# Tokens to the experts and back: row tables in DRAM with indirect transfers instead of products with selection matrices

## The chip, the cores and the metric

The kernel runs on one core of one Trainium2 chip; the other cores do nothing. The metric is the device time of one execution in microseconds. Before the change the median of three runs is 1745.82 us (1745.56 to 1750.58).

## What is computed

Two decoder layers over 256 tokens of width 1024. Each layer has a mixer (a state-space part, attention and a gated delta rule, with one projection in and one out), a layer norm, a feed-forward part and another layer norm. The feed-forward part is dense in layer 0 (width 3584). In layer 1 it is a mixture of 8 experts of the same size, and each token goes to its two best:

```python
def swiglu(x, w_gate, w_up, w_down):
    return (jax.nn.silu(x @ w_gate) * (x @ w_up)) @ w_down

def moe_ffn(x, router_w, w_gate, w_up, w_down):
    logits = (x @ router_w).astype(F32)
    top_val, top_idx = lax.top_k(logits, TOP_K)
    gates = jax.nn.softmax(top_val, axis=-1)
    combine = jnp.sum(jax.nn.one_hot(top_idx, N_EXPERTS, dtype=F32) * gates[..., None], axis=-2)
    out = jnp.zeros(x.shape, F32)
    for e in range(N_EXPERTS):
        out = out + combine[..., e:e + 1] * swiglu(x, w_gate[e], w_up[e], w_down[e]).astype(F32)
    return out.astype(x.dtype)
```

The layer ends with `layer_norm(DEEPNORM_ALPHA * x + f, ...)`, where `f` is this output.

## The kernel before

Each engine has its own program, and all order between them is written out by hand with semaphores. The change lies in the expert part of layer 1, and in one place of SP's queue in layer 0.

**The channel mixer** (one function per engine, each named `channel_mixer`) runs once for the dense layer (`i is None`, both blocks of 128 tokens) and once per expert `i` (one block of at most 128 gathered tokens). The weights of a layer or an expert come in 42 pieces of 1 MB (`SEQ`): for each of 7 strips `j` of 512 hidden columns two gate pieces (G), two up pieces (U) and, one strip later, two down pieces (D). SP loads piece `r` into one of 7 raw buffers (`next_piece`, L415) as soon as the low part of the piece seven before it has been taken. A float32 weight is used as a sum of two parts: ScalarE writes the high part (`high_part`, L581), VectorE the low part as raw minus high (`low_part`, L950), each into one of three buffers that become free when TensorE has used the piece three before. TensorE makes three products (high by high, low by high, high by low) for each pair of tiles: `inward` (L1361) for G and U, `outward` (L1373) for D; for an expert that is 12 products of 128x512 per piece. After the gate pieces ScalarE takes silu (L612), VectorE multiplies with the up product to `h` (L982), TensorE turns it with four transposes (L1435), and ScalarE and VectorE write its two parts (L618, L1005).

**The router** (L1244 to L1275) finds each token's two experts, their weights (`comb`) and each token's place among those of its expert (`pos`, from products with a triangle of ones, L1751 to L1755). `count_i` holds the largest number of tokens of an expert; only if it is over 128 a second pass over the experts runs.

**Tokens to an expert.** VectorE compares a row of 0..127 with `pos` and gets a selection matrix `pick` (L957). TensorE multiplies the two parts of x (`xs`, written by L770 and L1229) with it, 16 products per part (`gather`, L1344), which gives the expert's tokens already turned; ScalarE and VectorE copy them out as `xg` (L590, L963). For expert i+1 both gathers stand inside expert i, the first after piece 35, the second after piece 39. TensorE also turns `pick` once per expert (L1443), and ScalarE copies it (L621).

**Back to the tokens.** At an expert's end ScalarE and VectorE write two parts of its output (`ye`, L603, L988), TensorE multiplies them with the turned `pick` (8 products, L1458), and VectorE adds the result times `comb` to x (L996). x was scaled by ALPHA before, on POOL (L569). The last layer norm follows (L927 to L939).

**SP's queue in layer 0** (L433 to L438): the mixer's weights, the first 7 pieces of the dense layer (`first_pieces`, L410; pieces 4 and 5 wait until half of the output projection has been used, piece 6 until the projection is done), then pieces 7 to 41, then the mixer's weights of layer 1.

## Time and profile before

| | |
|---|---|
| median of three runs | 1745.82 us |
| profiled execution: its time, its span | 1748.89 us, 1746.7 us |
| TensorE busy | 1638.8 us (94%) |
| VectorE busy | 1297.2 us (74%) |
| ScalarE busy | 935.4 us (54%) |
| POOL busy | 155.4 us (9%) |
| mean granted TensorE clock | 0.968 of 2.4 GHz |
| moved by DMA | 440.14 MB, mean 252 GB/s |

An engine's busy time is a mean over stages that are limited by different things. The dense layer takes TensorE from 227 to 464 us, the experts from 709 to 1731 us. In rows of a timeline the columns are start, duration, engine, line, operation, output and input, count, and in brackets the idle time before with what ended it. A row of busy time by windows has the stretch, its length, the busy time (instructions) of PE, PEld, DVE, ACT and POOL, the granted clock, the DMA share and GB/s. PEld is TensorE's weight load, SPq an issue of SP's DMA queue. A TensorE clock of 1.00 is 2.4 GHz, of 0.50 is 1.2 GHz.

### The profile page before, as it was taken

What the parts mean: (1) busy time and instruction counts of PE and PEld (TensorE: products, weight loads), DVE (VectorE), ACT (ScalarE), POOL (GpSimd) and SP (SyncE); (2) the same over time, 40 slices, a digit from 0 to 9 for tenths busy, and PEclk for the clock granted to TensorE, in tenths of its full rate; (3) what the DMA queues carried; (4) which work ended last, traced back from release to release, by engine and by line L of the source; (5) the groups of instructions that cost most, each with busy time, mean ns of one, the idle gap of its engine ahead of it and who ended that gap; (6) DMA issues with size and microseconds to landing.
All of it is one profiled execution on the core that took longest, in us unless ns stands there. A gap on an engine that the chain in (4) does not pass through costs nothing.

```text
span 1746.7 us, 23280 instructions
## 1 busy us (share of the span) xinstructions
PE 1638.8 (94%) x8938; PEld 1330.4 (76%) x8938; DVE 1297.2 (74%) x1219; ACT 935.4 (54%) x778; POOL 155.4 (9%) x169
## 2 busy tenths in 40 slices
PE   7978989999899697999999999999999999999996
PEld 6857578888787474788788788787887887887885
DVE  7776655444528566588888888888888888887886
ACT  1233234433202421577676776777776776776773
POOL 0342074000015211000000000000000000000000
PEclk9988999999999898899999999999999999999998
DMA  8430156554443104599899899898998998998991
GB/s 315 146 121 3 49 194 216 192 177 162 162 146 125 44 3 169 178 375 360 298 374 359 294 374 343 324 376 315 353 372 319 337 371 322 350 373 295 365 378 51
DMA packets 183982, 440.14 MB, mean 252 GB/s; under 512 B 6576, under 2 KB 8752, under 8 KB 183152
## 3 DMA queue, kind: packets, MB, share of 16 engines
q1 hardware_dynamic: 182640, 431.15, 68.4%
q0 software_dynamic: 1280, 8.15, 1.2%
q8 instruction: 41, 0.67, 0.2%
q14 instruction: 21, 0.17, 0.0%
HBM read 438.22 MB, written 1.05 MB: 251 GB/s over the span
## 4 chain that ended last, share of the span: by engine, by line
PE 81%; DVE 11%; ACT 4%; issue 4%; DMA 1%; DVEq 0%; SPq 0%
PE ps L1361 41%; PE ps L1373 21%; PE ps L1320 5%; PE ps L1680 3%; PE ps L1344 2%; PE ps L1435 2%; ACT hi L581 2%; DVE arena L1053 1%; PE ps L1327 1%; PE ps L1458 1%; PE ps L1650 1%; DMA arena<-in_w_in 1%; PE ps L1636 1%; DVE small L927 1%; DVE arena L907 1%
## 5 line engine op out<-in xcount | busy, mean ns | idle before, releaser
L950 DVE TENSOR_TENSOR lo<-arena,hi 128x2048 fp32r<-128x2048 f32 x378 | 871.3, 2307 | 254.6 <-ACT hi L581 254.5
L581 ACT ACTIVATE hi<-arena 128x2048 fp32r<-128x2048 f32 x378 | 723.9, 1918 | 421.2 <-PE ps L1361 291.0
L1361 PE MATMUL ps<-hi,xg 128*128 128x512 f32 x1792 | 557.8, 393 | 1.5 <-DVE xg L963 1.5
L1361 PEld LDWEIGHTS ps<-hi,xg 128*128 128x128 f32 x1792 | 337.4, 189 | 71.4 <-issue 1.7
L1361 PE MATMUL ps<-lo,xg 128*128 128x512 f32 x896 | 350.3, 391 | 0.0
L1373 PE MATMUL ps<-hi,hTe 128*128 128x512 f32 x896 | 282.5, 396 | 0.7
L1361 PEld LDWEIGHTS ps<-lo,xg 128*128 128x128 f32 x896 | 169.3, 189 | 35.9
L1373 PEld LDWEIGHTS ps<-hi,hTe 128*128 128x128 f32 x896 | 164.0, 188 | 33.4 <-issue 1.6
L1373 PE MATMUL ps<-lo,hTe 128*128 128x512 f32 x448 | 175.0, 391 | 0.0
L1361 PE MATMUL ps<-hi,xs 128*128 128x512 f32 x448 | 138.8, 391 | 0.5 <-issue 0.5
L1320 PE MATMUL ps<-arena 128*128 128x256 f32 x544 | 121.6, 386 | 3.9 <-DMA arena<-in_w_in 2.8
L1320 PEld LDWEIGHTS ps<-arena 128*128 128x128 f32 x544 | 105.4, 194 | 19.9 <-issue 4.6
L1373 PEld LDWEIGHTS ps<-lo,hTe 128*128 128x128 f32 x448 | 84.2, 188 | 18.8
L1361 PEld LDWEIGHTS ps<-hi,xs 128*128 128x128 f32 x448 | 84.4, 189 | 18.2 <-issue 0.9
L1361 PE MATMUL ps<-lo,xs 128*128 128x512 f32 x224 | 87.4, 390 | 0.0
L643 ACT ACTIVATE arena<-ps 128x512 f32<-128x512 f32 (+2 forms) x22 | 12.3, 558 | 124.3 <-PE ps L1320 98.8
L1373 PE MATMUL ps<-hi,hTd 128*128 128x512 f32 x224 | 69.5, 391 | 0.0
L1680 PE MATMUL ps<-arena 128*128 128x512 f32 x128 | 58.1, 602 | 2.6 <-DVE arena L1157 2.6
L982 DVE TENSOR_TENSOR arena<-ps,arena 128x512 f32<-128x512 f32 (+1 forms) x63 | 46.9, 744 | 5.7 <-PE ps L1361 5.7
L1361 PEld LDWEIGHTS ps<-lo,xs 128*128 128x128 f32 x224 | 42.2, 188 | 8.8
L1373 PEld LDWEIGHTS ps<-hi,hTd 128*128 128x128 f32 x224 | 41.6, 188 | 8.3
L1680 PEld LDWEIGHTS ps<-arena 128*128 128x128 f32 x128 | 23.3, 190 | 29.2 <-issue 24.9
(327 smaller groups left out, 1509.5 us busy)
## 6 DMA issues: line engine op xcount, KB each, us to landing
arena<-in_mg SPq DMA_DIRECT2D x112, 1024.0 KB, 5.1
arena<-in_mu SPq DMA_DIRECT2D x112, 1024.0 KB, 5.2
arena<-in_md SPq DMA_DIRECT2D x112, 1024.0 KB, 5.0
arena<-in_w_in SPq DMA_DIRECT2D x8, 2048.0 KB, 10.3
arena<-in_wg SPq DMA_DIRECT2D x14, 1024.0 KB, 5.2
arena<-in_wu SPq DMA_DIRECT2D x14, 1024.0 KB, 5.1
arena<-in_wd SPq DMA_DIRECT2D x14, 1024.0 KB, 5.0
arena<-in_w_out SPq DMA_DIRECT2D x4, 2048.0 KB, 7.7
```

The costliest lines, as they stand in the source:

```text
L581: af(hi[r % PARTS][:, :], raw[r % RAWS], ACT.Copy).then_inc(hi_ready, 1)
L907: ins = v_.tensor_tensor_scan(mt[2 * k + 1][:, jj * T:(jj + 1) * T], rad, mt[2 * k][:, jj * T:(jj + 1) * T], 0.0, ALU.mult, ALU.add)
L927: step(v_.bn_stats(stats[:, 6 * c:6 * c + 6], xc))
L950: tt(lo[r % PARTS][:, :], raw[r % RAWS], hi[r % PARTS][:, :].bitcast(F32), ALU.subtract)\
L982: tt(hh[:, 0:512 * nb], ps[:, 4 + nb:4 + 2 * nb, :].rearrange("p a n -> p (a n)"), sg[:, 0:512 * nb], ALU.mult).then_inc(h_ready, 1)
L1053: ins = stt(qkv[:, c, :], cin[:, c, w:w + T], cw[:, c, w:w + 1], qkv[:, c, :], ALU.mult, ALU.add)
L1320: ins = mm(ps[:, bank, col:col + T], w[:, k, c0:c0 + P], xT[:, k, :], start=(k == 0), stop=(k == KT - 1))
L1344: ins = mm(ps[:, bank + k // 4, (k % 4) * P:(k % 4 + 1) * P], xs[part][:, b * D + k * P:b * D + (k + 1) * P], pick[:, b, :], start=(b == 0 ...
L1361: ins = mm(ps[:, (4 if w == "G" else 4 + nb) + b, :], tok[a][:, kk * nt + b * P:kk * nt + (b + 1) * P], tiles_of(part[r % PARTS], r)[:, k, ...
L1373: ins = mm(ps[:, 2 * b + c, :], hT[j % 2][a][:, h0:h0 + P], tiles_of(part[r % PARTS], r)[:, q, 512 * c:512 * (c + 1)], start=(j == 0 and p ...
L1435: ins = tr(ps[:, h_bank(i, j) + b, q * P:(q + 1) * P], hh[:, 512 * b + q * P:512 * b + (q + 1) * P], ident)
L1680: return mm(ps[:, (0, 1, 2, 5)[bank_at], :], xT[:, k, b * P:(b + 1) * P], wo[k // 4][:, k % 4, 512 * c:512 * (c + 1)], start=first, stop=f ...
```

## The change

Two tables of 17 x 128 rows of 1024 floats in DRAM, `xg_rows` and `y_rows`, hold the experts' tokens and the experts' outputs. Expert i owns rows 128 i to 128 i + 127.

- SP fills both tables with zeros, in two transfers from a new input of zeros, between the first 7 pieces of the dense layer and the rest.
- The router gives each token two row numbers (`row_of`) instead of `pos` and `comb`.
- POOL scatters x into `xg_rows` with four indirect transfers of 128 rows (two choices, two blocks), and then scales x by ALPHA.
- SP loads an expert's 128 rows into `xg_in` (for expert 0 before the stream of pieces, for the next ones after piece 16 of the running expert). TensorE turns them with 8 transposes (`tokens_turned`), ScalarE copies the high part, and VectorE subtracts it for the low part. The gathers, `pick`, its turned form and the parts `xs` of layer 1's x are gone.
- At an expert's end ScalarE copies the output as plain float32 and issues a transfer of it to the expert's rows of `y_rows`. This now stands behind the last high part of that turn. The 8 products back, the second part of `ye` and the additions to x inside the expert are gone.
- After the last expert's store has landed, POOL gathers each token's two rows with four indirect transfers, and VectorE adds them to x with their weights, in four passes of 1024 elements; then the last norm runs as before.

```diff
@@ -418,14 +422,26 @@
...
+            def tokens_of(i):
...
+                rows = xg_rows[bass.ds(i * P, P), :] if not isinstance(i, int) else xg_rows[i * P:(i + 1) * P, :]
+                sp.dma_start(xg_in, rows).then_inc(xg_loaded, 16)
...
+                        if r == TOKENS_AT:
+                            sp.wait_ge(xg_psum, i + 1)
+                            tokens_of(i + 1)
+                last = first + NE - 1
...
-                    next_piece(first + NE - 1, r, *expert_weights(NE - 1))
+                    next_piece(last, r, *expert_weights(NE - 1))
+                    if r == TOKENS_AT:
+                        sp.wait_ge(xg_psum, last + 1)
+                        tokens_of(last + 1)
...
@@ -433,10 +449,15 @@
...
             first_pieces(0, *dense)
+            for rows, done in ((xg_rows, xg_zeroed), (y_rows, y_stored)):
+                sp.dma_start(rows.rearrange("(n p) d -> p n d", p=P), zeros.unsqueeze(1).to_broadcast([P, ROWS // P, D]))\
+                    .then_inc(done, 16)
             for r in range(RAWS, NP):
                 next_piece(None, r, *dense)
             load_mixer(1)
             first_pieces(1, *expert_weights(0))
+            sp.wait_ge(x_scattered, 64)
+            tokens_of(0)
...
@@ -564,9 +585,21 @@
...
+            pool.wait_ge(xg_zeroed, 16)
+            pool.wait_ge(rows_ready, 1)
+            for k in range(2):
+                for b in range(NB):
+                    pool.indirect_dma_start(xg_rows, bass.IndirectOffsetOnAxis(ap=row_of[:, 2 * k + b:2 * k + b + 1], axis=0),
+                                            x[:, b, :], None).then_inc(x_scattered, 16)
...
-            pool.wait_ge(xs_lo, 4 + NB)
-            pool.tensor_scalar(x, x, ALPHA, None, ALU.mult).then_inc(sc_added, 1)
+            pool.wait_ge(x_scattered, 64)
+            pool.tensor_scalar(x, x, ALPHA, None, ALU.mult).then_inc(x_scaled, 1)
+            pool.wait_ge(y_all, 1)
+            for b in range(NB):
+                for k in range(2):
+                    pool.indirect_dma_start(y_in[:, b, k, :], None, y_rows,
+                                            bass.IndirectOffsetOnAxis(ap=row_of[:, 2 * k + b:2 * k + b + 1], axis=0))\
+                        .then_inc(y_gathered[b], 16)
...
@@ -594,13 +627,6 @@
...
-                    if r == NP - 1 and i is not None:
-                        for c in range(2):
-                            if c == 0:
-                                act.wait_ge(down_part, i + 4)
-                            else:
-                                act.wait_ge(piece_used, at(i, NP, NP))
-                            af(ye[0][:, 512 * c:512 * (c + 1)], ps[:, c, :], ACT.Copy).then_inc(ye_hi, 1)
...
@@ -616,11 +642,19 @@
...
-                    if i is not None and r == AT["G", 1, 1]:
-                        act.wait_ge(pickt_psum, i + 1)
-                        af(pickT[:, :], ps[:, 7, 0:T], ACT.Copy).then_inc(pickt_evac, 1)
...
+                    if i is not None and r == NP - 1:
+                        act.wait_ge(y_stored, i * 16 + 16)
+                        for c in range(2):
+                            if c == 0:
+                                act.wait_ge(down_part, i + 4)
+                            else:
+                                act.wait_ge(piece_used, at(i, NP, NP))
+                            af(ye[:, 512 * c:512 * (c + 1)], ps[:, c, :], ACT.Copy).then_inc(ye_ready, 1)
+                        act.wait_ge(ye_ready, i * 2 + 2)
+                        rows = y_rows[i * P:(i + 1) * P, :] if isinstance(i, int) else y_rows[bass.ds(i * P, P), :]
+                        act.dma_start(rows, ye).then_inc(y_stored, 16)
...
@@ -950,17 +982,11 @@
...
-            def pick_tokens(i):
...
-                for b in range(NB):
-                    where = pos[:, b, i:i + 1] if isinstance(i, int) else pos[:, b, bass.ds(i, 1)]
-                    ts(pick[:, b, :], C("iota"), where, None, ALU.is_equal).then_inc(pick_ready, 1)
...
-                dve.wait_ge(xg_psum, at(i, 2, 2))
-                bank = 6 if i is None else 2
-                v_.tensor_copy(xg[1][:, :], ps[:, bank:bank + 2, :].rearrange("p a n -> p (a n)")).then_inc(xg_lo, 1)
+                dve.wait_ge(xg_hi, 1 if i is None else i + 2)
+                tt(xg[1][:, :], ps[:, 2:4, :].rearrange("p a n -> p (a n)"), xg[0][:, :].bitcast(F32), ALU.subtract)\
+                    .then_inc(xg_lo, 1)
...
@@ -981,32 +1007,13 @@
...
-                    if r == NP - 1 and i is not None:
-                        for c in range(2):
-                            dve.wait_ge(ye_hi, i * 2 + (c + 1))
-                            half = slice(512 * c, 512 * (c + 1))
-                            tt(ye[1][:, half], ps[:, c, :], ye[0][:, half].bitcast(F32), ALU.subtract)\
-                                .then_inc(ye_lo, 1)
-                        for k, bank in enumerate((2, 3, 7, 6)):
-                            c, b = divmod(k, 2)
-                            if k == 2:
-                                low_ahead(r)
-                            dve.wait_ge(sc_out, i * 4 + (k + 1))
-                            xc = x[:, b, 512 * c:512 * (c + 1)]
-                            stt(xc, ps[:, bank, :], comb[:, b, i:i + 1] if isinstance(i, int) else
-                                comb[:, b, bass.ds(i, 1)], xc, ALU.mult, ALU.add).then_inc(sc_added, 1)
-                        dve.wait_ge(sc_added, i * 4 + 5)
-                    else:
-                        low_ahead(r)
+                    low_ahead(r)
...
-                    if i is not None and r == AT["G", 1, 1]:
-                        dve.wait_ge(pickt_psum, i + 1)
-                        pick_tokens(i + 1)
...
@@ -1259,27 +1261,29 @@
...
-            step(tt(oh1, oh1, b8(g1), ALU.mult))
-            step.then(tt(oh2, oh2, b8(g2), ALU.mult))
-            for e0 in (0, NE):
-                step(tt(comb[:, :, e0:e0 + NE], oh1, oh2, ALU.add))
-            step(v_.memset(comb[:, :, 16:17], 0.0))
-            step(v_.memset(pos[:, :, 16:17], -1.0))
...
-            step.then(stt(t8, ps[:, 1, 0:16].rearrange("p (b e) -> p b e", b=2), 1000.0, sel_, ALU.add, ALU.mult))
-            step(ts(pos[:, :, 0:NE], t8, -1000.0, None, ALU.add))
-            step(ts(pos[:, :, NE:2 * NE], t8, -1000.0 - P, None, ALU.add))
+            rank = ps[:, 1, 0:16].rearrange("p (b e) -> p b e", b=2)
...
+            step.then(ts(t8, rank, float(P), float(P * (NE - 1)), ALU.is_ge, ALU.mult))
+            step.then(tt(t8, t8, rank, ALU.add))
+            step.then(stt(t8, rev, -float(P), t8, ALU.mult, ALU.add))
+            step(tt(lg, oh1, t8, ALU.mult))
+            step.then(tt(l2, oh2, t8, ALU.mult))
+            step(v_.tensor_reduce(m1, lg, AX_X, ALU.add))
+            step.then(v_.tensor_reduce(m2, l2, AX_X, ALU.add))
+            step(ts(row_of[:, 0:2], m1, float(P * NE), None, ALU.add))
+            ts(row_of[:, 2:4], m2, float(P * NE), None, ALU.add).then_inc(rows_ready, 1)
+            step.wait()
+            dve.wait_ge(rows_ready, 1)
...
-            pick_tokens(0)
...
-            dve.wait_ge(sc_added, 1)
...
+            dve.wait_ge(y_stored, 16 * (NE + 1))
...
@@ -1287,6 +1291,13 @@
...
+                dve.wait_ge(y_stored, 16 * (2 * NE + 1))
+            v_.memset(m1, 0.0).then_inc(y_all, 1)
+            dve.wait_ge(x_scaled, 1)
+            for b in range(NB):
+                dve.wait_ge(y_gathered[b], 32)
+                step.then(stt(x[:, b, :], y_in[:, b, 0, :], g1[:, b:b + 1], x[:, b, :], ALU.mult, ALU.add))
+                step.then(stt(x[:, b, :], y_in[:, b, 1, :], g2[:, b:b + 1], x[:, b, :], ALU.mult, ALU.add))
...
@@ -1330,20 +1341,13 @@
...
-            def gather(i, part):
...
-                if part == 0:
-                    pe.wait_ge(pick_ready, at(i, 2, 2))
-                    if i is not None:
-                        pe.wait_ge(sc_added, i * 4 + 1)
-                elif i is not None:
-                    pe.wait_ge(xg_hi, at(i, 1, 1))
-                bank = 6 if i is None and part else 2
+            def tokens_turned(n, loaded):
...
+                pe.wait_ge(xg_loaded, loaded)
+                if n is not None:
+                    pe.wait_ge(xg_lo, n)
...
-                    for b in range(NB):
-                        ins = mm(ps[:, bank + k // 4, (k % 4) * P:(k % 4 + 1) * P],
-                                 xs[part][:, b * D + k * P:b * D + (k + 1) * P], pick[:, b, :],
-                                 start=(b == 0), stop=(b == NB - 1))
+                    ins = tr(ps[:, 2 + k // 4, (k % 4) * P:(k % 4 + 1) * P], xg_in[:, k * P:(k + 1) * P], ident)
...
@@ -1437,27 +1439,8 @@
...
-                    if r == AT["G", 1, 1]:
-                        pe.wait_ge(sc_added, i * 4 + 1)
-                        for b in range(NB):
-                            ins = tr(ps[:, 7, b * P:(b + 1) * P], pick[:, b, :].bitcast(F32), ident)
-                        ins.then_inc(pickt_psum, 1)
...
-                        gather(i, 0)
-                    if r == AT["D", FC - 2, 1]:
-                        gather(i, 1)
-                if i is None:
-                    return
-                pe.wait_ge(pickt_evac, i + 1)
-                pe.wait_ge(xg_lo, i + 2)
-                pe.wait_ge(ht_lo, at(i, FC, FC))
-                for k, bank in enumerate((2, 3, 7, 6)):
-                    c, b = divmod(k, 2)
-                    pe.wait_ge(ye_lo, i * 2 + (c + 1))
-                    for part in range(2):
-                        ins = mm(ps[:, bank, :], pickT[:, b * P:(b + 1) * P], ye[part][:, 512 * c:512 * (c + 1)],
-                                 start=(part == 0), stop=(part == 1))
-                    ins.then_inc(sc_out, 1)
+                        tokens_turned(i + 1, i * 16 + 32)
...
```

SP's queue as the dense layer starts; the last row of `first_pieces` is piece 6 (in_wu), and below it come pieces 7, 8 and 9. Before:

```order
L410 DMA arena<-in_wu 128x4x512 x2
L410 DMA arena<-in_wg 128x4x512 x2
L410 DMA arena<-in_wu 128x4x512
L419 DMA arena<-in_wu 128x4x512
L419 DMA arena<-in_wd 128x2x1024 x2
```

After:

```order
L414 DMA arena<-in_wg 128x4x512 x2
L414 DMA arena<-in_wu 128x4x512
L453 DMA xg_rows<-in_zeros 128x17x1024
L453 DMA y_rows<-in_zeros 128x17x1024
L423 DMA arena<-in_wu 128x4x512
L423 DMA arena<-in_wd 128x2x1024 x2
L423 DMA arena<-in_wg 128x4x512 x2
```

Two DMAs of 128x17x1024 stand between piece 6 and piece 7; nothing else has moved there.

TensorE at the end of an expert's turn of the loop. Before, the products back (L1458, with the two parts of `ye`) and the branch:

```order
L1456 REGISTER_ALU
L1458 MATMUL ps<-ye_65,pickT 128x512
L1458 MATMUL ps<-ye_66,pickT 128x512
L1458 MATMUL ps<-ye_65,pickT 128x512
L1458 MATMUL ps<-ye_66,pickT 128x512
L1456 REGISTER_ALU
L1458 MATMUL ps<-ye_65,pickT 128x512
L1458 MATMUL ps<-ye_66,pickT 128x512
L1458 MATMUL ps<-ye_65,pickT 128x512
L1458 MATMUL ps<-ye_66,pickT 128x512
L1760 REGISTER_ALU
L1760 COMPARE_AND_BRANCH
```

After, the last products of the last D piece (L1377) and the branch:

```order
L1377 MATMUL ps<-lo_54,hTe_61 128x512
L1377 MATMUL ps<-hi_51,hTe_61 128x512
L1377 MATMUL ps<-hi_51,hTe_62 128x512
L1377 MATMUL ps<-lo_54,hTe_61 128x512
L1741 REGISTER_ALU
L1741 COMPARE_AND_BRANCH
```

The eight products and their waits are gone, and the next expert's first product follows the last D product.

ScalarE at the same place. `hi` is a high part, `ye` or `arena<-ps` an output copy; `hi_51` is here the high part of piece 2 of the next expert. Before:

```order
L581 ACTIVATE hi_50<-arena 128x2048
L600 REGISTER_ALU
L603 ACTIVATE ye_65<-ps 128x512
L602 REGISTER_ALU
L603 ACTIVATE ye_65<-ps 128x512
L580 REGISTER_ALU
L581 ACTIVATE hi_51<-arena 128x2048
L780 REGISTER_ALU
L780 COMPARE_AND_BRANCH
L581 ACTIVATE hi_49<-arena 128x2048
```

After:

```order
L614 ACTIVATE hi_51<-arena 128x2048
L648 ISA
L651 REGISTER_ALU
L654 ACTIVATE arena<-ps 128x512
L653 REGISTER_ALU
L654 ACTIVATE arena<-ps 128x512
L655 ISA
L657 ISA
L657 DMA y_rows<-arena 128x1024
L812 REGISTER_ALU
L812 COMPARE_AND_BRANCH
L614 ACTIVATE hi_49<-arena 128x2048
```

The two output copies went from ahead of this high part to behind it, and the issue of the store stands between them and the branch, behind a wait for the copies.

## Rows read from the trace of the kernel before

**Rows 1.** The page's chain that ended last, by line.

```profile
PE ps L1361 41%; PE ps L1373 21%; PE ps L1320 5%; PE ps L1680 3%; PE ps L1344 2%; PE ps L1435 2%; ACT hi L581 2%; DVE arena L1053 1%; PE ps L1327 1%; PE ps L1458 1%; PE ps L1650 1%; DMA arena<-in_w_in 1%; PE ps L1636 1%; DVE small L927 1%; DVE arena L907 1%
```

**Rows 2.** Busy time by windows; last columns: granted clock, DMA share, GB/s.

```profile
741.00:813.00 72.00, 72.00 (x327) 59.55 (x326) 63.44 (x36) 53.68 (x34) 0.00 (x0) 1.00 1.02 375
221.00:231.00 10.00, 5.20 (x20) 4.57 (x21) 6.02 (x9) 1.49 (x3) 4.33 (x25) 0.66 1.02 397
```

**Rows 3.** The source line that turns the selection (durations in ns min/median/max).

```profile
L1443 PE MATMUL ps<-cst,pick x16: 270/271/276, 729.1 to 1624.1; 128*128 128x128 f32 x16
```

**Rows 4.** Chain of waits in expert 0: start, us, what.

```profile
757.70 10.88 PE ps L1361 x48
...
771.30 0.44 PE ps L1435 x4
```

**Rows 5.** Timeline of TensorE at one boundary, and the groups by form.

```profile
955.03 0.39 PE L1373 MATMUL ps<-lo,hTe 128*128 128x512 f32 x1
...
957.22 0.70 PE L1373 MATMUL ps<-hi,hTe 128*128 128x512 f32 x2
...
965.12 2.76 PE L1458 MATMUL ps<-ye,pickT 128*128 128x512 f32 x8 [2.21 <-DVE ye L988]
...
967.69 1.05 PE L1361 MATMUL ps<-hi,xg 128*128 128x512 f32 x2
...
L1435 PE MATMUL ps<-cst,arena 128*128 128x128 f32 x224 | 33.7, 273 | 4.8 <-DVE arena L982 4.8
```

**Rows 6.** Timeline of ScalarE, then of VectorE, at that boundary.

```profile
963.44 1.90 ACT L581 ACTIVATE hi<-arena 128x2048 fp32r<-128x2048 f32 x1
...
965.36 1.28 ACT L581 ACT_TABLE_LOAD   x1
...
976.25 1.28 ACT L612 ACT_TABLE_LOAD   x1
...
957.40 2.29 DVE L950 TENSOR_TENSOR lo<-arena,hi 128x2048 fp32r<-128x2048 f32 x1 [0.32 <-ACT hi L581]
...
959.61 1.22 DVE L963 CAST xg<-ps 128x1024 fp32r<-128x1024 f32 x1
```

**Rows 7.** Timeline of SP's queue as the dense layer starts.

```profile
218.62 0.37 SPq L410 DMA_DIRECT2D arena<-in_wu  x1
...
219.58 1.43 SPq L419 DMA_DIRECT2D arena<-in_wd  x2
```

**Rows 8.** DMA issues between 215 and 222 us: KB each, us to landing.

```profile
arena<-in_wd SPq DMA_DIRECT2D x2, 1024.0 KB, 11.0
```

**Rows 9.** Timeline of TensorE in the dense layer.

```profile
272.73 0.62 PE L1373 MATMUL ps<-hi,hTd 128*128 128x512 f32 x2
```

**Rows 10.** DMA issues of the page.

```profile
x<-in_x_in SPq DMA_DIRECT2D x2, 512.0 KB, 4.5
...
out<-x SPq DMA_DIRECT2D x2, 512.0 KB, 2.6
...
cst<-in_consts POOLq DMA_DIRECT2D x1, 6.0 KB, 4.2
```

**Rows 11.** Timeline from the router to expert 0.

```profile
683.51 0.59 POOL L565 DMA_DIRECT2D score_rows<-in_ln  x1 [59.19 <-DVE x L939]
...
686.02 1.95 PE L1310 MATMUL ps<-cst,x 128*128 128x128 f32 x8
...
699.72 0.15 DVE L1275 CAST count_i<-rt 128x1 int32<-128x1 f32 x1
...
704.23 1.02 ACT L590 ACTIVATE xg<-ps 128x1024 fp32r<-128x1024 f32 x1 [7.39 <-PE ps L1344]
...
709.11 1.22 PE L1361 MATMUL ps<-hi,xg 128*128 128x512 f32 x2 [1.51 <-DVE xg L963]
```

**Rows 12.** Timeline at the end of the last expert.

```profile
1729.38 0.60 ACT L603 ACTIVATE ye<-ps 128x512 fp32r<-128x512 f32 x1 [0.76 <-PE ps L1373]
...
1734.88 1.29 DVE L927 BATCH_NORM_STATS2 small<-x 128x6 f32<-128x512 f32 x2 [1.54 <-issue]
```

More of the change, by code:

```diff
@@ L22 @@
 I32 = mybir.dt.int32
+U32 = mybir.dt.uint32
 AX_X = mybir.AxisListType.X
@@ L39 @@
 NE = 8
+ROWS = 17 * P
 ALPHA = float((2 * L) ** 0.25)
@@ L58 @@
 RAWS, PARTS = 7, 3
+TOKENS_AT = 16
 SEQ = [(w, 0, p) for w in "GU" for p in range(2)]
@@ L140, with build @@
 O_KV, O_KG, O_KD, O_UP, O_WT, O_VP, O_O, O_ST = 3072, 4608, 5376, 6144, 6912, 7680, 8448, 3072
-def build(nc, x_in, w_in, w_out, consts, params, s5_b, glu_w, ln, wg, wu, wd, mg, mu, md, out):
+def build(nc, x_in, w_in, w_out, consts, params, s5_b, glu_w, ln, wg, wu, wd, mg, mu, md, zeros, xg_rows, y_rows, out):
     ctx = ExitStack()
@@ L171, in build @@
         count_i = sb("count_i", 2, I32)
-        pos = sb("pos", 2 * 17)[:, :].rearrange("p (b e) -> p b e", b=2)
-        comb = sb("comb", 2 * 17)[:, :].rearrange("p (b e) -> p b e", b=2)
+        row_of = sb("row_of", 4, U32)
         rt = sb("rt", 160)
@@ L246, in build @@
         hT_e = [[parts(f"hTe{i}{q}", A_HT + 1024 * i + 512 * q, 512) for q in range(2)] for i in range(2)]
-        ye = [parts(f"ye{q}", A_HT + 2048 + 1024 * q, 1024) for q in range(2)]
+        ye = arena[:, A_HT + 2048:A_HT + 2048 + D]
+        xg_in = arena[:, A_XS:A_XS + D]
+        y_in = arena[:, A_RAW:A_RAW + 4 * D].rearrange("p (b k d) -> p b k d", b=2, k=2)
         xg = [parts(f"xg{q}", A_XT + D * q, D) for q in range(2)]
@@ L250, in build @@
         hh = arena[:, A_H:A_H + 1024]
-        pick = parts("pick", A_PK, T)[:, :].rearrange("p (b s) -> p b s", b=2)
-        pickT = parts("pickT", A_PK + T, T)
         def sm(a, n):
@@ L317, in build @@
             sem(n) for n in ("lg_psum", "gate_exp_in", "gate_exp", "sel_ready", "pos_psum", "route_ready"))
-        pick_ready, pickt_psum, pickt_evac = (sem(n) for n in ("pick_ready", "pickt_psum", "pickt_evac"))
-        xg_psum, xg_hi, xg_lo, ye_hi, ye_lo, sc_out, sc_added = (
-            sem(n) for n in ("xg_psum", "xg_hi", "xg_lo", "ye_hi", "ye_lo", "scatter_psum", "scatter_added"))
+        xg_zeroed, rows_ready, x_scattered, x_scaled, xg_loaded = (
+            sem(n) for n in ("xg_zeroed", "rows_ready", "x_scattered", "x_scaled", "xg_loaded"))
+        xg_psum, xg_hi, xg_lo = (sem(n) for n in ("xg_psum", "xg_hi", "xg_lo"))
+        ye_ready, y_stored, y_all = sem("ye_ready"), sem("y_stored"), sem("y_all")
+        y_gathered = [sem(f"y_gathered_{b}") for b in range(NB)]
         out_ready, out_stored = sem("out_ready"), sem("out_stored")
@@ L583, in gathered @@
             def gathered(i):
-                act.wait_ge(xg_psum, at(i, 2, 1))
                 if i is None:
-                    act.wait_ge(lg_psum, 1)
+                    act.wait_ge(xg_psum, 1)
                 else:
+                    act.wait_ge(xg_psum, i + 2)
                     act.wait_ge(piece_used, at(i, NP, AT["U", FC - 1, 1] + 1))
@@ L768, in _ @@
             for b in range(NB):
-                act.wait_ge(x_ready, 2 * NB + b + 1)
-                af(xs[0][:, b * D:(b + 1) * D], x[:, b, :], ACT.Copy).then_inc(xs_hi, 1)
                 for q in range(4 - 2 * b):
@@ L1755, in _ @@
             mm(ps[:, 1, 16:24], C("ones"), sel_[:, 8:16], start=False, stop=True).then_inc(pos_psum, 1)
-            pe.wait_ge(xs_lo, 4 + NB)
-            gather(None, 0)
-            gather(None, 1)
+            tokens_turned(None, 16)
             with pe.Fori(0, NE) as i:
@@ L1809 @@
     arr["glu_w"] = np.asarray(s5_glu_w).reshape(L, 2, P, S5W).transpose(0, 2, 1, 3).reshape(L, P, 512)
+    arr["zeros"] = np.zeros((P, D), f32)
     arr["ln"] = np.stack([np.stack([np.asarray(g)[l], np.asarray(b)[l]]) for l in range(L)
@@ L1812 @@
     nc = bacc.Bacc("TRN2", target_bir_lowering=False, num_devices=1)
-    order = ("x_in", "w_in", "w_out", "consts", "params", "s5_b", "glu_w", "ln", "wg", "wu", "wd", "mg", "mu", "md")
+    order = ("x_in", "w_in", "w_out", "consts", "params", "s5_b", "glu_w", "ln", "wg", "wu", "wd", "mg", "mu", "md", "zeros")
     sent, args = {}, []
@@ L1818 @@
         args.append(nc.dram_tensor(f"in_{name}", a.shape, mybir.dt.from_np(a.dtype), kind="ExternalInput").ap())
+    for name in ("xg_rows", "y_rows"):
+        args.append(nc.dram_tensor(name, (ROWS, D), F32, kind="Internal").ap())
     out = nc.dram_tensor("out_0", (1, T, D), F32, kind="ExternalOutput").ap()
```

6 lines of the change are left out of this document (removed).

## Prediction

> **What bounds the kernel now.** I read the page's chain of waits first, then stretches of the expert stage by windows, then one expert boundary instruction by instruction, then the DMA queue of SP at the places where the change adds transfers. The profiled execution took 1748.89 us, of which 1746.7 us are its span, and its sum is what I work on; the median of the runs shown is 1745.82 us, 3.1 us less.
> The chain that ended last runs 62% through the two lines of the channel mixer, L1361 and L1373 [rows 1]. So inside an expert a microsecond less of TensorE's queue is a microsecond less of time. The second resource is DMA: its share reads 1.02 at 375 GB/s in the steady part of an expert, and 397 GB/s is the most it moved in any longer stretch [rows 2]. The other engines have room there: in 72.00 us VectorE is busy 63.44 and ScalarE 53.68 [rows 2].
>
> **The expert stage, 8 times.** From the first to the last turning of the selection (16 instructions, 2 per expert, 729.1 to 1624.1 us [rows 3]) there are 7 periods, so one is 895.0/7 = 127.9 us. Its floor: 42 pieces of 12 products are 504; 48 take 10.88 us [rows 4], 0.2267 each, together 114.2 us. Seven groups of four transposes take 0.44 each, 3.1 us. What is over, 10.6 us, is what the change touches:
> - Two gathers with the selection matrix, 16 products each. From the start of the last product before one to the first after it, 955.03 to 957.22 us [rows 5], are 2.19 us, 1.96 more than between two products; 3.9 us go.
> - The turned selection matrix, 2 transposes: 0.2 us goes.
> - The boundary, the remaining 6.5 us: TensorE waits for the second half of the expert's output (2.21 us idle, after a wait of its weight load), does 8 scatter products (2.76 us at this boundary), and starts the next expert at the lower clock, a pair of products taking 1.05 instead of 0.70 us; then it waits for h before the first transposes, 4.8 us in all 7, 0.7 each [rows 5].
> New on TensorE are 8 transposes of the loaded token rows, at 0.11 each 0.9 us.
> The boundary doesn't become free. There the high and low parts of the weights come just in time: TensorE finishes piece r, ScalarE then needs 1.92 us for the high part of r+3 and VectorE 2.29 for the low part [rows 6], 4.3 of the 5.44 us that two pieces take. After the change ScalarE does at the end of an expert, in this order: a high part (1.9), two output copies (0.6 each), the issue of the store (0.4, as on SP [rows 7]), the loop's end and the table load of 1.28 us [rows 6]: it is free 5.1 us after the last product. The high part of piece 3 could have begun after 2.7 us, so it is 2.4 us late; 1.1 of that is slack, 1.3 is stall. The second table load, before the first silu [rows 6], delays the parts of piece 5 and with them h, which stands behind them on VectorE: 0.9 us more. The new token subtraction (1.22 us, behind the low part of 2.29 in one piece's time [rows 6]) costs about 0.3. I take 2.5 us of stall. A period is then 114.2 + 3.1 + 0.9 + 2.5 = 120.7 us, 7.2 less; 7 of them give 50, the last expert, whose end belongs to the tail, 3.9 - 0.9 = 3. Together **-53 us**. Ends: stall 0 gives -71, and 6 us, the whole of what the boundary costs now, gives -28.
>
> **The zero fill.** Two tables of 2176 rows of 4 KB, 17.83 MB, are filled from DRAM to DRAM on SP's queue, behind piece 6 of the dense layer (issued at 218.62) and ahead of pieces 7 to 9 (the last issued by 221.0) [rows 7]. The queue is served in its order: the last of those pieces need 11.0 us to land instead of 5 [rows 8]. Piece 8 is the first D piece, whose product starts at 272.73 us; piece 7 is used 5.44 earlier, at 267.3 [rows 9]. Its two parts take 4.3 us and the piece itself 4 us of moving and landing. So the fill, which starts moving at about 222, is hidden up to 259: **37 us of cover**, and beyond it each microsecond is lost, as the dense layer is TensorE's afterwards. No row of before shows a DRAM to DRAM transfer. At the highest rate of a load, 397 GB/s [rows 2], it takes 45 us (stall 8); if reading and writing share that rate, 90 us (stall 53). A half megabyte written to DRAM lands in 2.6 us and one read in 4.5 [rows 10]; 34 such steps one after another would be 88 and 153 us, but most of each is latency that a long transfer pays once. The nearest row is the streamed load, and I take 52 us, a little slower since both sides are DRAM: **+15 us**, with the ends +8 and +53 kept.
> The Trainium skill, page "DMA: Bandwidth & Descriptors", section "Latency and other measured facts", speaks against this: copies between HBM tensors ran at 207 GB/s per direction at a row pitch of 512 KiB, which is the pitch between the 17 rows that a partition writes here. By it the fill takes 86 us and the stall is 49; no run here shows it, and it would make the sum positive (first rival).
>
> **The router.** Before: the count is cast at 699.72, 16+16 gather products and two casts follow, and the first product of expert 0 starts at 709.11 [rows 11]. After: some 8 more small VectorE steps of 0.2 us until 700.9; POOL issues 4 indirect scatters, at 0.6 us (its plain issue [rows 11]) or more, I take 1.0, so the last is out at 704.9; a small POOL transfer lands 4.2 us after its issue starts [rows 10], at 708; SP reads back half a megabyte, 2.6 to 4.5 us, take 3.5; 8 transposes at the lower clock 1.95, ScalarE's copy 1.02 [rows 11], VectorE's subtraction 1.22, semaphores 0.3. That is 717: **+8 us** (3 to 15; the issue of an indirect transfer is the unknown). Pieces 7 to 9 of expert 0 are queued behind SP's wait, but have 20 us until they are used.
>
> **The tail.** Before: last output copy at 1729.38, the final norm starts at 1734.88 [rows 12]. After: copies done at 1730.0, the store lands 3.0 later, the branch on the count costs the 1.5 us idle that it costs now, 1734.5; two gathers issued by 1736.5 and landed at 1740, two more at 1742; VectorE adds 2 x 1.28 per block (as a pass over 1024 elements takes), so the norm starts at 1745: **+10 us** (5 to 18).
>
> **Sum.** -53 + 15 + 8 + 10 = -20; 1748.9 - 20 = 1729, and less the 3.1 that the profiled execution was above the median, 1726 us.
>
> **Rivals.**
> 1. The fill at half the rate, 86 to 90 us: stall 50 instead of 15, sum +15 to +18, 1762 us, slower. It decides from a fill of about 72 us on. For it: every byte passes DRAM twice. Against it: nothing in the trace but that DMA engines load at 397 GB/s, where reading and writing also both happen.
> 2. The expert stage gives back half: either the boundary stall stays at 6 us, or DMA becomes the limit. Demand is 42 pieces of 1.05 MB plus 1.05 MB of token rows in 120.7 us, 373 GB/s, against 397 seen [rows 2]; a limit of 360 makes the period 125. Gain 27 instead of 53: 1752 us.
> The Trainium skill, page "HBM Reference", section "Specifications (TRN2)", puts the share of a core at about 358 GB/s, and above that when it streams alone. With 358 the period is 126 and the time 1763; the trace's 375 GB/s over 72 us disagrees [rows 2], so it weighs little here.
> 3. The fill doesn't hold up the pieces (its packets go beside theirs, or it issues without blocking the engines' rings): stall near 0, 1711 us.
>
> **Chances.** Forecast 0.50, first rival 0.28, second 0.12, third 0.07, rest 0.03. A measurement of this kernel tells 0.3%, 5 us, from no change. The forecast's own range is 1708 to 1742. Faster: nearly all of forecast and third, 0.55; within 0.3%: the edge of the forecast and half of the second rival, 0.09; slower: the first rival and the rest of the second, 0.36. Eight times in ten: 1704 to 1770.
>
> **What would show it.** In the profile after: a DMA pair of 8.9 MB on SP's queue at 219 us and one gap of TensorE at about 267 us, as long as the fill less 37 us (the first step; a gap of 50 is the first rival, none the third). Periods of the token transposes of 120 to 121 us with no gap of TensorE over 2 us at a boundary (second step; periods of 125 with ScalarE waiting for DMA would be the second rival). First product of expert 0 some 8 us after where it stood relative to the router's one-hot steps, and 15 us from the last product to the final norm instead of 5.5. I am wrong at the root if ScalarE's high parts begin to wait for loads inside an expert, or if POOL needs several microseconds per indirect transfer.

## The result, and the profile after

The changed kernel takes **1759.65 us** (median of 5 runs, 1756.72 to 1760.34); the ratio to the kernel before is 1.0055, with a 95% interval of 1.0041 to 1.0069. It is slower by half a per cent; the two medians alone are 13.8 us apart, and the kernel before scatters from 1744.73 to 1750.58 us. 1726 us and "faster" were forecast; the range (1704 to 1770) holds the time, the sign was wrong. The profiled execution has a span of 1758.2 us against 1746.7. These 11.5 us are a sum of four parts, each read between the same two instructions in both traces:

| part | forecast | measured | read from |
|---|---|---|---|
| zero fill | +15 | +25.2 | start of the router's 8 transposes: 686.02 [rows 11], now 711.21 us |
| router | +8 | +6.4 | from there to expert 0's first product: 23.1, now 29.45 us |
| expert stage | -53 | -37.0 | from that product to the last `ye` copy: 1020.3, now 983.3 us |
| tail | +10 | +16.6 | from that copy to the last norm: 5.5 [rows 12], now 22.1 us |
| sum | -20 | +11.2 | the rest of 11.5 lies behind the norm |

**Fill.** TensorE's timeline in the dense layer (start, us, what, in brackets the idle time before and its releaser), then the second fill on SP's queue, the DMA issues of that stretch (KB each, us to landing) and two windows with the columns of [rows 2]:

```profile
266.66 0.39 PE L1365 MATMUL ps<-lo,xs 128*128 128x512 f32 x1
289.99 1.22 PE L1365 MATMUL ps<-hi,xs 128*128 128x512 f32 x2 [22.95 <-DVE lo L982]
```

```profile
219.60 14.71 SPq L453 DMA_DIRECT2D y_rows<-in_zeros  x1
```

```profile
xg_rows<-in_zeros SPq DMA_DIRECT2D x1, 8704.0 KB, 33.7
y_rows<-in_zeros SPq DMA_DIRECT2D x1, 8704.0 KB, 61.2
```

```profile
222.00:262.00 40.00, 36.41 (x163) 30.53 (x164) 15.80 (x12) 11.36 (x9) 33.56 (x80) 0.92 1.01 334
...
770.00:840.00 70.00, 70.00 (x318) 57.93 (x317) 62.14 (x34) 51.90 (x35) 0.00 (x0) 1.00 1.03 381
```

There is one gap, where it was foretold. The releaser named is VectorE's low part, but it only passes the wait on: the list of waits has ScalarE waiting for the piece that is queued behind the fill (engine, line, what it waited for: us in total, times, longest).

```profile
ACT hi L614 <- DMA arena<-in_wu: 33.9, 1, 33.9
```

The second transfer was issued at 219.60 us and landed 61.2 later, at 280.8. In the trace the first packet of the fills starts at 222.7 us, behind piece 6, and the last one ends at 280.0: 17.83 MB in 57.3 us, 311 GB/s, with a load of 1 MB on POOL's queue beside it. Start to start the gap costs 23.1 us. Behind it the clock is low (granted 0.69 from 262 to 300 us, a first pair of 1.22 us instead of 0.62): the nine products up to 293.68 us take 3.7 us instead of 2.0. That leads to 24.8 of the 25.2 us; the last 0.4 are open.

**Expert stage.** The wait at 981.12 us returns in every expert (858.09, 981.12, 1104.03, to 1472.84), every 122.95 us, which is the period; 127.9 before. The sixth interval, to 1597.38, is 124.5 us, since it has a stretch of low clock (the eight products from 1474.32 us on take 3.4 us instead of 1.8). The seventh, to 1718.24, is 120.9: at that boundary the two stalls shown below are missing. The stretch from one expert's last pieces to the next one's sixth, on TensorE, then on ScalarE and VectorE:

```profile
978.91 0.39 PE L1377 MATMUL ps<-lo,hTe 128*128 128x512 f32 x1
981.12 0.70 PE L1377 MATMUL ps<-hi,hTe 128*128 128x512 f32 x2 [1.82 <-DVE hTe L1015]
...
996.36 0.73 PE L1365 MATMUL ps<-hi,xg 128*128 128x512 f32 x2 [1.38 <-DVE lo L982]
...
1002.48 0.66 PE L1437 MATMUL ps<-cst,arena 128*128 128x128 f32 x4 [0.36 <-DVE arena L1008]
```

```profile
976.13 1.92 ACT L614 ACTIVATE hi<-arena 128x2048 fp32r<-128x2048 f32 x1
977.95 0.57 ACT L644 ACTIVATE hTe<-ps 128x512 fp32r<-128x512 f32 x1
978.08 2.29 DVE L982 TENSOR_TENSOR lo<-arena,hi 128x2048 fp32r<-128x2048 f32 x1 [0.35 <-ACT hi L614]
980.29 0.68 DVE L1015 TENSOR_TENSOR hTe<-ps,hTe 128x512 fp32r<-128x512 f32 x1
...
988.69 1.07 ACT L654 ACTIVATE arena<-ps 128x512 f32<-128x512 f32 x2
989.92 0.34 ACTq L657 DMA_DIRECT2D y_rows<-arena  x1
990.77 1.28 ACT L614 ACT_TABLE_LOAD   x1 [1.02 <-issue]
992.07 3.72 ACT L614 ACTIVATE hi<-arena 128x2048 fp32r<-128x2048 f32 x2
```

The boundary has become what the prediction described: ScalarE's copies, issue, table load (it is free at 992.05 us, 5.2 behind the last product's end; 5.1 were forecast), and then a stall of 1.38 us and one of 0.36. New is the first wait. TensorE has used up everything it may do without the last strip of hT, and its low part is made only behind the parts of a weight piece: 1.92 and 0.57 us on ScalarE, 2.29 and 0.68 on VectorE. The list of waits has it in all 8 experts:

```profile
PE ps L1377 <- DVE hTe L1015: 14.6, 8, 1.9
```

The seventh boundary, into the last expert, which stands outside the loop, shows one thing that the stall of 1.38 us hangs on. ScalarE issues the store there too, but loads no table and ends no turn of the loop:

```profile
1604.96 1.06 ACT L654 ACTIVATE arena<-ps 128x512 f32<-128x512 f32 x2
1606.20 0.34 ACTq L657 DMA_DIRECT2D y_rows<-arena  x1
1606.77 3.79 ACT L614 ACTIVATE hi<-arena 128x2048 fp32r<-128x2048 f32 x2 [0.74 <-ACT arena L654]
```

The high part begins 1.8 us behind the start of the copies, 3.4 at the boundary above, and TensorE has no stall behind it.

**Router and tail.** Timelines of all engines; `DMA_INDIRECT` is POOL's issue of a transfer by row numbers.

```profile
724.90 1.05 POOL L592 DMA_INDIRECT xg_rows<-x,row_of  x1 [14.88 <-DVE row_of L1276]
...
728.79 0.95 POOL L592 DMA_INDIRECT xg_rows<-x,row_of  x1 [0.31 <-issue]
732.61 0.34 SPq L428 DMA_DIRECT2D arena<-xg_rows  x1
...
736.06 1.97 PE L1350 MATMUL ps<-cst,arena 128*128 128x128 f32 x8 [13.61 <-DMA arena<-xg_rows]
...
740.66 1.22 PE L1365 MATMUL ps<-hi,xg 128*128 128x512 f32 x2 [2.63 <-DVE xg L988]
...
1723.97 0.60 ACT L654 ACTIVATE arena<-ps 128x512 f32<-128x512 f32 x1 [0.70 <-PE ps L1377]
1724.60 0.35 ACTq L657 DMA_DIRECT2D y_rows<-arena  x1
...
1733.18 0.06 DVE L1295 MEMSET rt<- 128x2 f32 x1 [13.95 <-issue]
1733.51 1.03 POOL L600 DMA_INDIRECT arena<-y_rows,row_of  x1 [995.39 <-DVE rt L1295]
...
1740.77 1.28 DVE L1299 SCALAR_TENSOR_TENSOR x<-arena,rt,x 128x1024 f32<-128x1024 f32 x1 [7.53 <-DMA arena<-y_rows,row_of]
...
1746.05 1.29 DVE L959 BATCH_NORM_STATS2 small<-x 128x6 f32<-128x512 f32 x2
```

An indirect issue holds POOL for 1.0 us, the value taken, with 1.3 from one to the next. In the tail the last store landed after 4.8 us, at 1729.4, and VectorE passed its memset only at 1733.18: behind the wait for the store stand the read of the count and the branch on it, 3.8 us in which nobody works.

### The profile page after: what moved, and what is told of

Same layout as the page of the kernel before. It is cut to its first block, busy times and chain, and to the rows that moved or that the text cites. A ratio compares the mean times of both kernels' runs of the same rounds, so it can differ in the third digit from the quotient of the medians.

```text
span 1758.2 us, 22567 instructions
## 1 busy us (share of the span) xinstructions
PE 1591.7 (91%) x8642; PEld 1287.0 (73%) x8642; DVE 1257.9 (72%) x1156; ACT 930.5 (53%) x768; POOL 155.3 (9%) x177
## 4 chain that ended last, share of the span: by engine, by line
issue 58%; PE 27%; DVE 10%; another core or an unknown queue 2%; ACT 2%; DMA 1%; POOL 0%; POOLq 0%; SPq 0%; DVEq 0%; ACTq 0%
PE ps L1365 8%; PE ps L1331 5%; PE ps L1377 4%; PE ps L1663 3%; DVE arena L1060 1%; PE ps L1338 1%; PE ps L1633 1%; DMA arena<-in_w_in 1%; DVE small L959 1%; DVE arena L939 1%; PE ps L1619 1%; DVE x L967 1%; DVE x L971 1%; PE ps L1629 0%
## 5 line engine op out<-in xcount | busy, mean ns | idle before, releaser
L1377 PE MATMUL ps<-hi,hTe 128*128 128x512 f32 x896 | 283.9, 398 | 14.6 <-DVE hTe L1015 14.6
L1377 PEld LDWEIGHTS ps<-hi,hTe 128*128 128x128 f32 x896 | 164.9, 189 | 49.9 <-DVE lo L982 17.8
L1377 PE MATMUL ps<-lo,hTe 128*128 128x512 f32 x448 | 175.8, 392 | 0.0
L1331 PEld LDWEIGHTS ps<-arena 128*128 128x128 f32 x544 | 106.6, 196 | 20.2 <-issue 4.6
L1377 PEld LDWEIGHTS ps<-lo,hTe 128*128 128x128 f32 x448 | 84.7, 189 | 18.8
L600 POOL DMA_INDIRECT arena<-y_rows,row_of x4 | 3.9, 964 | 996.3 <-DVE rt L1295 995.4
L1377 PE MATMUL ps<-hi,hTd 128*128 128x512 f32 x224 | 69.6, 392 | 0.0
L1663 PE MATMUL ps<-arena 128*128 128x512 f32 x128 | 58.1, 602 | 2.6 <-DVE arena L1164 2.6
L1377 PEld LDWEIGHTS ps<-hi,hTd 128*128 128x128 f32 x224 | 41.6, 188 | 8.3
```

The lines of the kernel that those rows point to most:

```text
L1331: ins = mm(ps[:, bank, col:col + T], w[:, k, c0:c0 + P], xT[:, k, :], start=(k == 0), stop=(k == KT - 1))
L1377: ins = mm(ps[:, 2 * b + c, :], hT[j % 2][a][:, h0:h0 + P], tiles_of(part[r % PARTS], r)[:, q, 512 * c:512 * (c + 1)], start=(j == 0 and p ...
L1663: return mm(ps[:, (0, 1, 2, 5)[bank_at], :], xT[:, k, b * P:(b + 1) * P], wo[k // 4][:, k % 4, 512 * c:512 * (c + 1)], start=first, stop=f ...
```

## The experiments

The theory: the fill stalls TensorE by its length less 37 us; taking gather 2 out gave nothing, because the wait for hT's low part stood right behind it; the tail pays for a read in series. The rivals are told with each run. The first four kernels are the kernel before with one thing changed, the others the changed kernel. Every ratio is to the kernel before run beside it, whose median was 1749.2 to 1750.0 us there.

**The fills alone, in the kernel before**, two and then one.

```diff
             first_pieces(0, *dense)
+            for rows in (xg_rows, y_rows):      # second kernel: (xg_rows,)
+                sp.dma_start(rows.rearrange("(n p) d -> p n d", p=P), zeros...)
```

> The kernel before, with nothing of the change but the two zero fills (17.83 MB) in their place on SP's queue. Theory (queue): the loads behind the fills wait for them, 37 us of that are covered, the trace of the changed kernel shows the second fill landed 61 us after its issue, so +25 us, in one gap of TensorE of about 23 us before piece 7 of the dense layer. Rival (the gap comes from something else that the change moved, such as POOL's or VectorE's work): no gap, under +5 us.

> The kernel before with one of the two fills (8.91 MB). Theory (queue with 37 us of cover): the fill takes about 31 us, less than the cover, so within 2 us of the kernel before, no gap in the dense layer. Rival (the cost goes with the bytes, by contention or a shared limit): half of the cost of both fills, about +12 us.

One fill: 1749.86 us, ratio 1.0001 (0.9988 to 1.0014); it landed after 34.9 us, inside the cover, and TensorE has no wait there. Both fills: 1775.6, ratio 1.0154 (1.0132 to 1.0176), +25.6 us against the 1749.96 of the kernel before, with the gap in the same place, in the list of waits:

```profile
PE ps L1367 <- DVE lo L956: 23.2, 1, 23.2
```

So the fill is hidden up to a cover and paid for beyond it. That it is paid microsecond for microsecond is checked at this one length only.

**One gather at a time, in the kernel before.** 14 of the 16 products are left out of gather 2 (the one at 955 us in [rows 5]), then of gather 1.

```diff
-                for k in range(KT):
+                for k in range(KT - 1 if part and i is not None else 0, KT):   # gather 1: part == 0
```

> The kernel before with 14 of the 16 products of each expert's second gather left out (the low part of the tokens is then incomplete); the first gather and all copies stay. Theory (cover): these products fill a wait of TensorE for the low part of the last strip's h, so leaving them out gives back nothing: within 3 us (0 to -2). Rival (what the prediction assumed, that they are on the path): 8 times 1.7 us, -13 us.

> The kernel before with 14 of the 16 products of each expert's first gather left out (the high part of the tokens is then incomplete). It stands where TensorE has its next piece ready, so both theories expect the products to be on the path: 8 times 1.5 to 1.7 us, -12 to -14 us. If it gives nothing either, the whole loss in the expert stage is of another kind.

Gather 2 short: 1749.47, ratio 0.9999 (0.9986 to 1.0012), nothing. Gather 1 short: 1737.53, ratio 0.9935 (0.9919 to 0.9951), 11 to 12 us. The same 112 products were left out of either. TensorE with gather 2 short:

```profile
956.91 0.33 PE L1344 MATMUL ps<-pick,xs 128*128 128x128 f32 x2
958.88 0.71 PE L1373 MATMUL ps<-hi,hTe 128*128 128x512 f32 x2 [1.64 <-DVE hTe L1005]
```

A wait of 1.64 us has taken the place of 14 products, which at 0.11 to 0.12 each took about as long. It could have been read ahead: the row stands in the view of VectorE from which [rows 6] are taken, just above the first one shown there. The low part of hT ends at 957.07 us, and TensorE's first product that needs it starts at 957.22 [rows 5]:

```profile
956.39 0.68 DVE L1005 TENSOR_TENSOR hTe<-ps,hTe 128x512 fp32r<-128x512 f32 x1
```

**hT's parts first.** In the changed kernel ScalarE and VectorE make the parts of hT's last strip ahead of those of the weight piece that stood before them.

```diff
                 for r in range(NP):
                     w, j, p = SEQ[r]
+                    if r == AFTER_H[-1] and i is not None:
+                        turned_high(r)          # ScalarE: copy of hT's high part
                     if r + PARTS < NP:
                         high_part(i, r + PARTS)
...
-                    low_ahead(r)                # VectorE
+                    if r != AFTER_H[-1] or i is None:
+                        low_ahead(r)            # else behind hT's low part
```

> The changed kernel with the two parts of the last strip's turned h written ahead of the high and low part of piece 41, on ScalarE and VectorE. Theory (the second gather hid this wait, now bare at 1.82 us per expert): the waits go in all 8 experts, -14.6 us against the changed kernel, 1745. Rival (the wait only moves to the last D piece, whose parts are now later): under -5 us.

1742.25 us, ratio 0.9956 (0.9941 to 0.9972); the span falls from 1758.2 to 1740.0, and no wait for hT is left in the list. Of these 18.2 us 16.5 lie in the expert stage (983.3, now 966.8) and 1.1 in the tail, where the last store landed after 3.3 us instead of 4.8. The period falls by 2.1 us, from 122.95 to 120.85 (983.80 to 1104.65, two experts' first products). That isn't the wait for hT alone: the boundary's first stall shrinks too, from 1.38 to 0.86 us, and a short new one stands at each expert's start.

```profile
983.80 0.72 PE L1373 MATMUL ps<-hi,xg 128*128 128x512 f32 x2 [0.22 <-DVE xg L993]
...
993.13 0.74 PE L1373 MATMUL ps<-hi,xg 128*128 128x512 f32 x2 [0.86 <-DVE lo L987]
```

Together they give about what the gather's removal should have brought.

**The fill at another place**: behind piece 3 of layer 0, at 105 us, where the queue has little to do.

```diff
+                    if l == 0 and r == 4:
+                        for rows, done in ((xg_rows, xg_zeroed), (y_rows, y_stored)):
+                            sp.dma_start(rows..., zeros...).then_inc(done, 16)
...
             first_pieces(0, *dense)
-            for rows, done in ((xg_rows, xg_zeroed), (y_rows, y_stored)):
-                sp.dma_start(...)
```

> The changed kernel with both fills moved ahead on SP's queue, behind the first four pieces of the dense layer (issued by 104 us) instead of behind the seventh. From there the queue has nothing to do for 95 us, and the fills take 60. Theory (queue): the gap of 23 us and the low clock behind it go, -25 us against the changed kernel, about 1735 us, faster than the kernel before. Rival (fills slow the engines wherever they run): less than half of it.

1736.93 us, ratio 0.9928 (0.991 to 0.9946); span 1734.7, 23.5 less. The fills landed after 38.4 and 64.4 us, no faster than before, and the gap is gone: at this place the same bytes cost nothing that shows, so it was the place in the queue.

**The count read before the wait.** VectorE reads the count while the last store is under way.

```diff
-            dve.wait_ge(y_stored, 16 * (NE + 1))
             most = dve.value_load(count_i[0:1, 0:1], min_val=0, max_val=T)
...
+            dve.wait_ge(y_stored, 16 * (NE + 1))
             v_.memset(m1, 0.0).then_inc(y_all, 1)
```

> The changed kernel with VectorE reading the count ahead of its wait for the last store instead of behind it. Theory (the read of the count, some 2 us, lies behind the store's landing in the tail): -2 to -3.5 us against the changed kernel, near 1757. Rival (the branch costs the time, not the read): 0.

1756.03 us, ratio 1.0035 (1.0022 to 1.0048); span 1754.2, 4.0 less. From the store's issue to the memset are 4.4 us, 8.6 before. The timed ratios alone hardly part (1.0041 to 1.0069 before the edit); the timeline does. The edit moves the branch together with the read, so it doesn't tell which of the two takes the 3.8 us.

```profile
1725.22 0.35 ACTq L657 DMA_DIRECT2D y_rows<-arena  x1
...
1729.64 0.06 DVE L1295 MEMSET rt<- 128x2 f32 x1 [9.82 <-DMA y_rows<-arena]
```

**All three edits together.**

> The changed kernel with all three edits: fills early, h's parts first, count read first. If each cost stands alone, the sum is -25 - 14.6 - 3 = -43 us, 1717 us, 1.8% faster than the kernel before. If taking one wait away uncovers another, less: above 1725.

**1714.26 us** (1713.22 to 1716.82), ratio 0.9794 (0.9777 to 0.9812). This beats the kernel before by 2% and the changed one by 2.6%. The spans nearly add up: 23.5 + 18.2 + 4.0 = 45.7 us singly, 43.3 together.

**The stores left out**, to see what sets the stall of 1.38 us at a boundary (there are six such stalls, not seven: the last boundary has none).

```diff
-                        act.dma_start(rows, ye).then_inc(y_stored, 16)
+                        if isinstance(i, int):      # the last expert alone
+                            act.dma_start(y_rows[i * P:(i + 1) * P, :], ye).then_inc(y_stored, 16)
```

> The changed kernel with the stores of the experts' outputs left out for experts 0 to 6 (only the last expert's is made; the result is not the reference's). It asks what sets the stall of 1.4 us of TensorE a little after each of the 7 boundaries (996.36 us in the changed kernel's trace). Theory: ScalarE's queue there, in which the store's issue (0.34 us) and the idle time around it (0.18 before, 0.51 behind it up to the table load) stand ahead of the high part of the next expert's piece 3. Without them that high part begins about 0.7 to 1.0 us earlier, the 7 stalls shrink from 1.4 to 0.4 to 0.7, and the kernel takes 5 to 7 us less: a span of 1752, 0.996 to 0.997 of its own time before the edit. Rival: the stall belongs to the loads (the store's 0.5 MB beside them, pieces landing 1 us later than before): then it disappears altogether at the stall and other waits for loads shrink too, 10 us or more. Second rival: VectorE's own queue (the token subtraction) sets it, and nothing is gained: 1758.

> The kernel with all three edits (fill early, hT's parts first, count read first), and the stores of experts 0 to 6 left out as well (the result is not the reference's). What is left of waits for VectorE's low part at its 7 boundaries is 5.3 us in 6 places. Theory (ScalarE's queue): most of these 5.3 go, 1714.3 becomes about 1710. Rival (contention of the stores with the loads): more than 8 us go. Second rival (VectorE's queue): nothing, 1714.

In the changed kernel: 1756.65 us, ratio 1.0053 (1.0035 to 1.0072), no difference that the timed runs can tell; the profiled span is 5.1 us less. In the kernel with the three edits: 1709.76 against 1714.26 us, ratio 0.9781 (0.9761 to 0.9801), where the intervals overlap too. The rows are clearer. In the changed kernel the stall shrinks by 1.0 us at the boundary, as ScalarE's high part comes 1.0 us sooner behind the copies, and the group of waits falls from 31.2 to 25.3 us, of which 23.0 are the fill's gap:

```profile
992.79 0.73 PE L1365 MATMUL ps<-hi,xg 128*128 128x512 f32 x2 [0.37 <-DVE lo L982]
```

```profile
PE ps L1365 <- DVE lo L982: 25.3, 7, 23.0
```

The expert stage still takes 982.3 us, 983.3 before the edit, because this execution has four stretches of low clock in it (granted 0.89 from 1095 to 1110 us, and again around 1347, 1593 and 1716) where the changed kernel's has one, and each costs about 1.6 us; 2.4 of the 5.1 us of span lie in the tail. In the kernel with the three edits, where the stage has no such stretch behind its start in either execution, it falls by 5.0 us (965.6, now 960.6), as the 5.3 us of waits said.

So it is ScalarE's queue that sets this stall: the wait didn't vanish, as it should if the loads did it, and it didn't stay, as it should if it were VectorE's. No engine waits for a load in the expert stage, and the seventh boundary has the store beside the loads and no stall. There the table load and the loop's end are missing, which brings the high part 1.6 us forward, where the store's issue is worth 1.0; a kernel without the table load was not run. Whether a store issued by another engine would keep this gain was not tried.

## Why the prediction was wrong

**The expert stage, -53 forecast and -37.0 measured, is the step that failed.** Its sentences were "Two gathers with the selection matrix, 16 products each" and "3.9 us go". Gather 1 went; gather 2 covered the wait for hT's low part, and nothing of it came back. I had asked what is late next at the boundary, where stalls stood in the trace, but not at gather 2, where none stood because work filled it. The period was 122.95 instead of 120.7. In it, start to start and less an ordinary step of 0.23, the wait for hT costs 1.98 us; the boundary's two stalls cost 1.53 and 0.5, 2.0 against the 2.5 taken; the 8 new transposes 0.8 against 0.9. With the 117.3 of products and other transposes this gives 122.1; the other 0.8 is products that run a little slower behind each stall and each group of transposes (the 18 products behind 981.12 take 4.18 us, where 4.08 is the steady pace), which my floor of 0.2267 each didn't have. Over 8 experts the wait for hT is 16 us, as much as the whole miss of this term; the smaller stalls at the boundary and the slower products about cancel. That the lower clock behind a boundary goes was in the sum, but it was read at one boundary: before, the granted clock was 0.79 for 8 us at four of the seven (from 836, 965, 1348 and 1603 us) and 1.00 at the other three.

**The zero fill, +15 forecast and +25.2 measured.** Mechanism and place were right; the sizes were off. From its first packet to its landing the fill took 58.1 us (222.7 to 280.8) where 52 were taken. The cover was 35.0 us instead of 37: piece 7 was due at 266.9 us, its first product started 9.2 behind the fill's landing (8.3 taken), and the fill began at 222.7 (222 taken). That makes the gap of 23.1; the rest is mostly the low clock behind it, which the forecast left out. The first rival's rate, half of the load's, is refuted: 311 GB/s is less than 397, but far more than half of it.
The Trainium skill, page "DMA: Bandwidth & Descriptors", section "Latency and other measured facts", gives 207 GB/s at a pitch of 512 KiB from one partition's row to the next. I applied it to the 512 KiB between the 17 rows of one partition; from partition to partition the rows of this fill are 4 KiB apart, so the page's case was not run here, and its figure is neither confirmed nor refuted.

**The router, +8 forecast and +6.4 measured**, was near, though its terms add up to 716 and not 717, so to +7. Issue (1.0 us each), landing (3.5), load back (3.5) and transposes (1.97) came as taken. Two misses about cancel, which is luck: the row numbers were ready 12.8 us behind the start of the transposes instead of 14.9 (a small VectorE step that took 1.95 us before, with POOL scaling x beside it, takes 0.18 now), and POOL was done issuing 5.7 us later instead of 4.0, as it issues one every 1.3 us.

**The tail, +10 forecast and +16.6 measured.** The store took 4.8 us to land instead of 3, and the "branch on the count" was priced at the 1.5 us of idle that it costs before; now 3.8 us stand in series behind the store. That the difference ran beside the last additions to x before is likely, but not shown. From the memset to the norm are 12.9 us, 10.5 in the forecast: block 0's second gather, issued at 1734.85, was used at 1740.77. So 1.8, 2.3 and 2.4 us make 6.5 of the 6.6 that were missing.

**The rivals.** The first said slower by a stall of 50 us; the kernel is slower with 25 us lost there, and -53 would have carried that. The second, half of the expert stage's gain given back, came nearer in size (27 said, 37.0 measured) but by neither of its ways: the boundary did shrink, and DMA isn't the limit, since no engine waits for a load in the expert stage at 381 GB/s. By 358 GB/s, the share of a core in the Trainium skill, page "HBM Reference", section "Specifications (TRN2)", the period would be 126; it is 122.95, at 367 GB/s from 983 to 1106 us. The same section of the Trainium skill says that a core streaming alone gets more than the share; the trace agrees, with 381 GB/s over 70 us. The third, a fill that holds nothing up, is refuted by the gap. The forecast of -20 was lost to hT (16 us), the fill (10) and the tail (7); without the first alone the kernel would still have been a little faster than before, as the run with hT's parts first is (span 1740.0 against 1746.7, ratio 0.9956). One end of the expert stage's range was added up wrongly: a stall of 6 us gives -29, not -28.

## What to carry to other kernels

Before work is counted as a gain, look at the row of every other engine that ends just as that work ends: a producer that finishes within its last fraction of a microsecond is a wait under cover, and removing the work buys next to nothing until the producer is moved. Bulk transfers that nobody waits for still hold up what is queued behind them; put them where the queue is idle, and price the place by the first queued piece that somebody needs. A read of a scalar and its branch belong ahead of a long wait, not behind it.

## What the runs showed of the hardware

- Two transfers from DRAM to DRAM, 17.83 MB in rows of 4 KB, ran at 311 GB/s with 1 MB loaded beside them, while loads reach 381 GB/s over 70 us. Issuing the second of the two held SP's queue for 14.7 us.
- Half a megabyte stored to DRAM landed in 2.6 us with nothing beside it [rows 10], in 8.6 (median of 7) between the streamed loads, and at the tail in 4.8, in 3.3 to 4.7 in the edited kernels with all stores, and in 2.6 and 3.2 with the stores of the other experts left out.
- An indirect transfer of 128 rows of 4 KB held POOL for 0.93 to 1.05 us, 1.24 to 1.35 us from one to the next; scatters landed in 3.5 us, gathers in 5.7.
- A short stretch of low clock (granted 0.50, 1.2 GHz, from 1474.3 to 1477.7 us; eight products in 3.4 us instead of 1.8) costs about 1.6 us. Two profiled executions can differ by several of them, so a difference of a few us between spans is read stage by stage.
